# A gated recurrence with its first level ahead of the states and block copies on ScalarE, and a routing with two spreads ahead of the first pick

## The reference, cut to what matters

```python
# per head (4 heads of 128), forward and backward; f = gate, k = 1 - f
S_t = diag(f_t) S_{t-1} + k_t v_t^T          # S_0 = final state of the context
o_t = S_t^T q_t                              # o = o_forward + o_backward
out = rmsnorm(o) * silu(g)
# then: x += g1 * (concat(hyena, out) @ w_out);  h = modulate(rmsnorm(x))
aff = softmax(h @ router_w)                  # (256 tokens, 16 experts)
gates, idx = top_k(aff.T, 32)                # each expert takes its 32 tokens
y = (silu(xg @ w1) * (xg @ w3)) @ w2         # per expert, times gates, added back
```

## Time and profile before

| | us |
|---|---|
| median of three runs | 2678.49 |
| the profiled execution | 2676.36 |
| its span | 2674.3 |
| TensorE busy | 2302.1 (86%) |
| VectorE busy | 774.6 (29%) |
| ScalarE busy | 344.9 (13%) |
| mean granted TensorE clock | 0.929 |

### The profile page before, as it was taken

One profiled execution on the slowest core, in us unless ns is written; L12 is line 12 of the kernel. 1 busy time (PEld: TensorE's weight loads), 2 busy tenths in 40 slices (PEclk: granted clock), 3 DMA queues, 4 the chain that ended last, 5 costly groups with the idle time before them and its releaser, 6 DMA issues.

```text
span 2674.3 us, 34093 instructions
## 1 busy us (share of the span) xinstructions
PE 2302.1 (86%) x14956; PEld 1619.0 (61%) x14968; DVE 774.6 (29%) x1473; ACT 344.9 (13%) x618; POOL 17.5 (1%) x21
## 2 busy tenths in 40 slices
PE   7999989999999999999999999896666666666675
PEld 5888768888888789888886878652121111111221
DVE  5544534574000465511023338640000000000000
ACT  3001222002000232111002211210000000000000
POOL 1000000000000000000000000000000000000000
PEclk9999999999999999999999999988887788887778
DMA  9889235886445240044442223489999999999997
GB/s 394 343 354 379 95 142 226 354 341 256 157 141 204 90 147 20 24 169 148 136 172 78 66 77 115 189 330 428 428 427 428 426 428 427 428 427 427 426 428 338
DMA packets 70098, 709.51 MB, mean 265 GB/s; under 512 B 7776, under 2 KB 7904, under 8 KB 8672
## 3 DMA queue, kind: packets, MB, share of 16 engines
q1 hardware_dynamic: 69984, 707.79, 65.6%
HBM read 706.71 MB, written 1.05 MB: 265 GB/s over the span
## 4 chain that ended last, share of the span: by engine, by line
PE 62%; DMA 30%; DVE 7%; ACT 1%; issue 1%; SPq 0%; DVEq 0%; ACTq 0%
DMA arena<-in_experts 27%; PE ps L691 11%; PE ps L698 11%; PE ps L708 11%; PE ps L757 5%; PE ps L875 4%; PE ps L1071 4%; PE ps L1282 2%; PE ps L1314 2%; DMA ring<-in_experts 2%; PE ps L664 1%; PE ps L1069 1%; PE ps L773 1%; PE ps L1247 1%; PE ps L787 1%
## 5 line engine op out<-in xcount | busy, mean ns | idle before, releaser
L1282 PE MATMUL ps<-arena 128*32 128x512 f32 x1376 | 211.8, 748 | 147.0 <-DMA arena<-in_experts 146.5
L691 PE MATMUL ps<-hT_sq,arena 128*128 128x256 f32 x1376 | 312.1, 380 | 4.1 <-ACT hT_sq L1391 2.9
L708 PE MATMUL ps<-hid,arena 128*128 128x256 f32 x1408 | 311.1, 379 | 0.2 <-DVE hid L1796 0.2
L698 PE MATMUL ps<-hT_sq,arena 128*128 128x256 f32 x1376 | 311.0, 379 | 0.0
L708 PEld LDWEIGHTS ps<-hid,arena 128*128 128x128 f32 x1408 | 267.4, 190 | 36.9 <-issue 0.6
L691 PEld LDWEIGHTS ps<-hT_sq,arena 128*128 128x128 f32 x1376 | 260.5, 190 | 45.5 <-issue 8.5
L698 PEld LDWEIGHTS ps<-hT_sq,arena 128*128 128x128 f32 x1376 | 261.4, 190 | 35.5
L1282 PEld LDWEIGHTS ps<-arena 128*32 128x32 f32 x1376 | 42.4, 124 | 310.6 <-DMA arena<-in_experts 226.0
L1363 ACT ACTIVATE arena<-ps 128x512 f32<-128x512 f32 (+4 forms) x147 | 89.1, 615 | 946.1 <-PE ps L1293 308.5
L1796 DVE TENSOR_TENSOR hid<-sil,ps 128x256 f32<-128x256 f32 x88 | 37.0, 421 | 560.4 <-ACT sil L1415 560.2
L1757 DVE CUSTOM_DVE_ANT_0 hT_sq<-arena 128x1024 f32<-128x1024 f32 x168 | 194.5, 1221 | 0.0
(11 more groups left out here) (370 smaller groups left out, 2184.0 us busy)
## 6 DMA issues: line engine op xcount, KB each, us to landing
arena<-in_experts SPq DMA_DIRECT2D x129, 2048.0 KB, 41.1
arena<-in_ada SPq DMA_DIRECT2D x96, 1024.0 KB, 9.7
ring<-in_experts SPq DMA_DIRECT2D x42, 2048.0 KB, 40.9
ring<-in_ring_w SPq DMA_DIRECT2D x51, 1024.0 KB, 5.1
arena<-in_ffn_gate SPq DMA_DIRECT2D x44, 1024.0 KB, 6.5
arena<-in_ffn_up SPq DMA_DIRECT2D x44, 1024.0 KB, 6.2
arena<-in_ffn_down SPq DMA_DIRECT2D x44, 1024.0 KB, 4.8
hT_sq<-in_experts SPq DMA_DIRECT2D x21, 2048.0 KB, 40.4
```

The source lines that it names most:

```text
L691: last = mm(ps[:, ft, 0:T], gate3[:, kt, ft * P:(ft + 1) * P], h3[:, kt, :], start=kt == 0, stop=kt == KT - 1)
L698: last = mm(ps[:, ft, T:2 * T], up3[:, kt, ft * P:(ft + 1) * P], h3[:, kt, :], start=kt == 0, stop=kt == KT - 1)
L708: last = mm(acc(m), down3[:, ft, m * P:(m + 1) * P], hid3[:, ft, :], start=False, stop=True, skip_group_check=True)
L1282: last = mm(ps[32 * n:32 * n + 32, part, :], e_xe[:, kt, :], w[:, (kt % 2) * SLOT + n * 512:(kt % 2) * SLOT + (n + 1) * 512], start=kt == ...
```

## The change

- `hyena_back` moves ahead of the last unit of `b2_in`, on TensorE and on ScalarE.
- The first level of both directions comes first on TensorE, ahead of the context's transposes, which go to banks 0 to 3. The states are made one by one after level 0's halves. The parts beside start at level 1; `beside(12)` and `(13)` stand behind the two halves of the crossing, `(14)` and `(15)` behind the two sums of squares, where the eight filler matmuls stood.
- Level 0 doesn't scale `g_K`; `g_E` is filled and copied by halves there, behind a wait for the transposes (`hg_ctx_t`). The last level doesn't update `g_E`, which holds the product of `g_q` and `g_F` instead.
- From level 6 on (`MASKED`), ScalarE takes the scores over by block copies, two of 32 or one of 64 columns a tile, instead of VectorE's masked copy.
- The crossing's part of the output matmuls comes last within a bank. The variances of the second bank are made between the heads. Sqrt's table is loaded by a dummy before the second bank, Exp's in norm 9.
- Routing: the row copy comes ahead of the large one on ScalarE, two spreads ahead of the first pick with fillers around them, and the other 14 within expert 0.

```diff
-        x_kt = ar(B1 + 12288, 2048).rearrange("p (d t c) -> p d t c", d=2, t=TT)
-        x_v = tiles(ar(B1 + 15360, 1024), HYW)
+        x_kt = ar(B1 + 17408, 2048).rearrange("p (d t c) -> p d t c", d=2, t=TT)
+        x_v = tiles(ar(B1 + 1024, 1024), HYW)
...
+        MASKED = 6
@@ TensorE, hgrn
+                pe.wait_ge(sem("hg_gates"), 2)
+                pe.wait_ge(sem("hy_mixed"), 4)
+                for d in range(2):
+                    level(d, g_k, lambda d: g_q)
+                pe.wait_ge(sem("b2_evac"), B2_FIRST)
                 for d in range(2):
                     for tt in range(TT):
                         for h in range(HGH):
+                            last = tr(ps[:, 2 - 2 * d + tt, h * P:(h + 1) * P], x_k[:, d, h, tt * P:(tt + 1) * P], ident)
+                        last.then_inc(sem("hg_ctx_t"), 1)
...
                 for lev in range(NLEV):
                     for d in range(2):
-                        pe.wait_ge(sem("hg_taken"), 2 * lev + d + 1)
+                        if lev < MASKED:
+                            pe.wait_ge(sem("hg_taken"), 2 * lev + d + 1)
+                        else:
+                            pe.wait_ge(sem("hg_copied"), 2 * (lev - MASKED) + d + 1)
                         pe.wait_ge(sem("hg_scaled"), 2 * lev + d + 1)
-                        level(d, lambda d: g_K[:, d], lambda d: g_Q[:, d])
-                        beside(2 + 2 * lev + d)
+                        level(d, g_K if lev else g_k, lambda d: g_Q[:, d])
+                        if lev == 0:
+                            state(d)
+                        else:
+                            beside(2 * lev - 2 + d)
...
                 for b in range(2):
                     pe.wait_ge(sem("hg_os"), 2 * b + 2)
                     mm(ps[:, 4 + b, :], ones, sq[:, b * 512:(b + 1) * 512], start=True, stop=True).then_inc(sem("hg_out"), 1)
-                keep_clock(6, 8)
+                    beside(14 + b)
@@ TensorE, routing and experts
+                keep_clock(7, 2)
+                pe.wait_ge(sem("e_rows"), 3)
+                spread(range(0, 2))
+                keep_clock(7, 12)
                 pe.wait_ge(sem("e_rows"), 4)
-                spread(range(0, 8))
...
-                            spread(range(8, NE))
+                            spread(range(2, NE))
@@ ScalarE, hgrn
+                for lev in range(MASKED, NLEV + 1):
+                    hb = 1 << lev - 1
+                    for d in range(2):
+                        act.wait_ge(sem("hg_level"), 2 * lev + d + 1)
+                        for tt in range(TT):
+                            src = ps[:, 4 + 2 * d + tt, :].rearrange("p (h s) -> p h s", s=P)
+                            for lo in range(0, P, 2 * hb):
+                                early, late = (slice(lo + hb * i, lo + hb * (i + 1)) for i in ((0, 1) if d == 0 else (1, 0)))
+                                last = copy(g_A[early, d, tt, :, late], src[early, :, late])
+                        last.then_inc(sem("hg_copied"), 1)
@@ VectorE, hgrn
+                        if lev < MASKED:
+                            taken(lev, d)
+                        else:
+                            dve.wait_ge(sem("hg_level"), 2 * lev + d + 1)
+                        last = tt_(cut(g_Q[:, d], late), cut(g_q, late), cut(g_F[:, d], late), ALU.mult)
+                        if lev > 0:
+                            last = tt_(cut(g_K[:, d], early), cut(g_k[:, d], early), cut(g_E[:, d], early), ALU.mult)
+                        last.then_inc(sem("hg_scaled"), 1)
...
+                        if lev == 0:
+                            dve.wait_ge(sem("hg_ctx_t"), 4)
+                            nc.vector.memset(cut(g_E[:, d], late), 1.0)
+                            done(cp(cut(g_E[:, d], early), cut(g_F[:, d], late)))
                         dve.wait_ge(sem("hg_scaled"), 2 * lev + d + 1)
-                        done(tt_(cut(g_E[:, d], early), cut(g_E[:, d], early), edge_l, ALU.mult))
+                        if 0 < lev < NLEV:
+                            done(tt_(cut(g_E[:, d], early), cut(g_E[:, d], early), edge_l, ALU.mult))
                         done(tt_(cut(g_F[:, d], late), cut(g_F[:, d], late), edge_e, ALU.mult))
+                        if lev == NLEV:
+                            last = tt_(g_E[:, d], g_q, g_F[:, d], ALU.mult)
```

More of the change, by code:

```diff
@@ L1100, in hgrn, with level, state @@
             def hgrn():
[L1102 to L1105, removed]
+                def level(d, kk, qq):
                     for tt in range(TT):
                         for h in range(HGH):
[L1108 to L1112, removed]
+                            last = mm(ps[:, 4 + 2 * d + tt, h * P:(h + 1) * P],
+                                      kk[:, d, h, tt * P:(tt + 1) * P], qq(d)[:, h, tt * P:(tt + 1) * P],
+                                      start=True, stop=True)
+                    last.then_inc(sem("hg_level"), 1)
+                def state(d):
+                    if d == 0:
+                        pe.wait_ge(sem("hg_ctx_kt"), 4)
                     for h in range(HGH):
@@ L1117, in hgrn @@
                     last.then_inc(sem("hg_state"), 1)
[L1118 to L1120 removed]
+                pe.wait_ge(sem("hg_gates"), 2)
[4 more added lines that the diff above has]
+                for d in range(2):
                     for tt in range(TT):
                         for h in range(HGH):
[L1123 to L1131, removed]
+                            last = tr(ps[:, 2 - 2 * d + tt, h * P:(h + 1) * P], x_k[:, d, h, tt * P:(tt + 1) * P], ident)
+                        last.then_inc(sem("hg_ctx_t"), 1)
                 for lev in range(NLEV):
                     for d in range(2):
[L1135 removed]
+                        if lev < MASKED:
+                            pe.wait_ge(sem("hg_taken"), 2 * lev + d + 1)
+                        else:
+                            pe.wait_ge(sem("hg_copied"), 2 * (lev - MASKED) + d + 1)
                         pe.wait_ge(sem("hg_scaled"), 2 * lev + d + 1)
[L1137 to L1138 removed]
+                        level(d, g_K if lev else g_k, lambda d: g_Q[:, d])
[3 more added lines that the diff above has]
+                            beside(2 * lev - 2 + d)
+                pe.wait_ge(sem("hg_copied"), 2 * (NLEV - MASKED) + 1)
                 for d in range(2):
@@ L1144, in hgrn @@
                                   g_Q[:, d, h, (1 - d) * P:(2 - d) * P], start=True, stop=True)
-                last.then_inc(sem("hg_cross"), 1)
-                pe.wait_ge(sem("hg_cross_s"), 1)
-                pe.wait_ge(sem("hg_taken"), 2 * NLEV + 2)
+                    if d == 1:
+                        last.then_inc(sem("hg_cross"), 1)
+                    beside(2 * NLEV - 2 + d)
+                pe.wait_ge(sem("hg_copied"), 2 * (NLEV - MASKED) + 2)
                 pe.wait_ge(sem("hg_scaled"), 2 * NLEV + 3)
[L1149 to L1156, removed]
-                        last = mm(o[:, (1 - d) * P:(2 - d) * P], g_v[:, d, e0], g_X[:, d, h, :],
-                                  start=False, stop=d == 1, skip_group_check=True)
-                    if h % 2:
-                        last.then_inc(sem("hg_out"), 1)
@@ new lines, in hgrn @@
+                for b in range(2):
+                    for h in (2 * b, 2 * b + 1):
+                        o, e0 = half(6, h), slice(h * P, (h + 1) * P)
+                        mm(o, g_S[0][:, h, :], g_E[:, 0, h, :], start=h % 2 == 0, stop=False, skip_group_check=True)
+                        mm(o, g_S[1][:, h, :], g_E[:, 1, h, :], start=False, stop=False, skip_group_check=True)
+                        for d in range(2):
+                            for tt in range(TT):
+                                mm(o[:, tt * P:(tt + 1) * P], g_v[:, tt, e0], g_A[:, d, tt, h, :],
+                                   start=False, stop=False, skip_group_check=True)
+                    pe.wait_ge(sem("hg_cross_s"), 1)
+                    for h in (2 * b, 2 * b + 1):
+                        for d in range(2):
+                            last = mm(half(6, h)[:, (1 - d) * P:(2 - d) * P], g_v[:, d, h * P:(h + 1) * P], g_X[:, d, h, :],
+                                      start=False, stop=d == 1, skip_group_check=True)
+                    last.then_inc(sem("hg_out"), 1)
@@ L1387, in norm @@
                 root(rstd[:, :])
+                if i == 9:
+                    f(small[:, 225:226], ones[:, 0:1], ACT.Exp)
                 if shift is not None:
@@ L1581, in hgrn @@
                     f(sq3[:, 2 * b:2 * b + 2, :], g_F[:, 0, 2 * b:2 * b + 2, :], ACT.Square).then_inc(sem("hg_os"), 1)
+                    if b == 0:
+                        f(small[:, 224:225], ones[:, 0:1], ACT.Sqrt)
                 for h in range(HGH):
```

36 lines of the change are left out of this document (18 added, 18 removed).

## The result

The changed kernel takes 2656.4 us in the median of four runs (2654.79 to 2657.76), beside 2678.57 for the kernel before on the same chip. The ratio is 0.9919, 95% interval 0.9905 to 0.9933: 22.2 us or 0.8% faster, 0.9 us from the forecast.

A forecast was written before the change was run, and what follows sets the result against it. The expert load stream, started by the first weight slot's release, was taken to bound the kernel. Recurrence 17.5 plus routing 6.4 less hole 1.0 gave 22.9 us, so about 2655.5 from 2678.5; range 2648 to 2665.

The forecast's parts named there:

- this change is worth exactly what it moves the first slot's release: Expert weight stream: the span ends a fixed 918 us after load 9's wait ends at 1756.62, unless the stream tears.
- if load 9 moves by 24 and the end by less, the stream was torn: Sign of being wrong, at the expert load stream: the give-back step would then fail.
- its own bounds: Forecast's bounds on start (7.5 to 11), routing (2.4 to 7.4) and hole (0 to 3): 2649 to 2663 us.
- Recurrence: Start, levels, outputs and roots of the gated recurrence: projection starts 17.5 us earlier, at 1692.8.
- rival 3: Levels 6 and 7: ScalarE's twelve block copies are dear, above 3.1 us each making the kernel slower; chance 0.03.
- Routing: First pick and first slot: earlier row copy, fewer spreads and fillers gain 6.4 us, bounds 2.4 to 7.4.
- after the pick of expert 1 the clock was down for a while too: Routing: reason for taking 6.4 us instead of the 7.4 of full clock throughout.
- Rival 1: Routing: clock stays at 1.2 GHz through the pick, only 2.4 of 6.4 us arrives, 2659.5; chance 0.14.
- What is given back: Expert 0: six more spreads and ranks (9.0 us) delay load 17, leaving a 1.0 us hole in the stream.
- 1.0 + p: Hole ahead of load 17 with the whole landing lead; p is the extra time from a slower TensorE clock.
- its wait grows from 3.08 to about 11: Expert 0: TensorE's wait for the gated product, in us, behind six more ranks on VectorE.
- Rival 2: Behind expert 0's wait TensorE restarts at half clock: hole 6 to 11 us, time 2660.5 to 2665.5; chance 0.14.

The follow-up runs named there:

- x11: Changed kernel with the context's transposes and states ahead of the first level, as before the change; 2665.14 us, ratio 0.9949.
- x6: Changed kernel with VectorE's masked copy at all levels, none of ScalarE's block copies; 2658.99 us, ratio 0.9926.
- x10: Kernel before with 23 filler matmuls in TensorE's two waits ahead of the recurrence's output matmuls; 2676.02 us, ratio 0.9995.
- x2: Kernel before with the routing part of the change alone; 2674.52 us, ratio 0.9988.
- x7: Changed kernel with expert 0's gated product ahead of the last four ranks on VectorE; 2652.05 us, ratio 0.9909.
- x3: Changed kernel with six spreads in place of the twelve routing fillers, leaving eight for expert 0; 2658.67 us, ratio 0.9925.
- x5: Changed kernel without its fourteen filler matmuls in the routing; 2661.59 us, ratio 0.9935.
- x12: The changed kernel measured once more, unaltered; 2656.63 us, ratio 0.9921.
- x4: Changed kernel with the fourteen spreads behind the second half of expert 0's matmuls instead of between the halves; 2662.74 us, ratio 0.9943.
- x8: Changed kernel with 24 filler matmuls between the last expert's four last slots; 2655.16 us, ratio 0.9914.
- x9: Changed kernel with both the edits of x7 and x8; 2652.97 us, ratio 0.9910.

## Why the prediction was right

**The bound held up to the last landing.** In all fourteen profiles load 191 lands 905.3 us behind load 9, plus the lag's excess over 39.2 where there is one, within 0.2 us. The end comes 12.3 to 15.6 behind that. So "this change is worth exactly what it moves the first slot's release", less the hole, is shown for the last landing; behind it up to 3.3 us depend on the clock.

**The signs that it named came.** The first level's mask starts 10.4 us earlier with respect to the gates' end (2.5 instead of 12.8 behind it), there are 20 masked copies instead of 28, and the outputs start without idle time at clock 1.00. One sign of being wrong came too: "if load 9 moves by 24 and the end by less, the stream was torn". It was torn, by 1.53, for which the sum had 1.0. The range is wider at its lower end than its own bounds give: the best of each, 22.9 + 1.6 + 1.0 + 1.0 = 26.5, lead to 2652, not 2649. The measured time lies within either.

**Recurrence, 17.5 forecast, 17.38 measured.** Level 1 at 1624.44 for 1624.1, outputs at 1678.96 for 1678.8, release of loads 2 to 5 at 1687.96 for 1687.7, projection at 1692.94 for 1692.8. The fill and copy of E took 0.85, for 0.9 taken. The block copies were 0.27 to 0.33 for 0.3, and rival 3 falls: it needed 3.1 each. x11 shows the order at the start as a cause (5.7), x6 the block copies (3.2), x10 the clock in the outputs (2.6). These make 11.5; that the other 5.9 come from the parts beside, the fill of E and the table load moved off the path is argued from the timelines, and no run undoes one of them alone.

**Routing, 6.4 forecast, 7.42 measured** (24.80 less 17.38). This term was too small by 1.0: the discount "after the pick of expert 1 the clock was down for a while too" was not due, and the bound for 2.4 GHz throughout, 7.4, is what came. Yet the discount was no mere caution: x2, x7 and x11, with the same fillers, lost 1.6 to 3.0 between load 8 and load 9. That the changed kernel lost none of it is in part luck. Rival 1 did not happen in the changed kernel; x3 and x5 show that it would have, without the fillers (load 9 at 1737.58 and 1737.29), 5.8 and 5.5 late, where its two bounds are 5.0 apart. x5 was 5.2 slower than the changed kernel; x3 only 2.3, since its profile has neither the hole nor the slow last slot (1.5 and 1.6 us).

**What is given back, 1.0 forecast, 1.53 measured.** The step's rule, 1.0 + p, holds: TensorE had 11.37 of work between the wait and load 17 instead of 10.94, so p = 0.4. The six ranks cost 8.9 (the restart came 29.41 behind load 9, before 20.50) for 9.0. One number within it was wrong: "its wait grows from 3.08 to about 11" measured 7.75. Its own terms give 9.3 (3.08 and 9.0, less 2.8 for the spreads). The other 1.5 is that the spreads ran at half clock from 1741 on (28 instructions in 8.17, where 16 took 3.71 before), so that part 1 ended later and more of the ranks lay under TensorE's own work. The sum is the same, since VectorE's end decides.

Rival 2 falls, for another reason than the prediction's. It argued that before, "after 3.08 us of waiting the whole 10.94 still passed near full speed". It didn't. The group behind the gated product starts at half clock in both kernels, and at full clock only in x7, behind a wait of 0.91. Before, a window behind the restart of the earlier trace rows and the end of the slow part:

```profile
1778.00:1779.00 1.00, 1.00 (x5) 0.86 (x5) 0.00 (x0) 0.60 (x1) 0.00 (x0) 0.50 1.08 459
```

```profile
1780.52 2.05 PE L1257 MATMUL ps<-con,vec 128*128 128x128 f32 x16
```

The changed kernel, and x7:

```profile
1762.00:1763.00 1.00, 1.00 (x6) 0.76 (x5) 0.00 (x0) 0.60 (x1) 0.00 (x0) 0.50 1.08 459
```

```profile
1765.06 2.05 PE L1271 MATMUL ps<-con,vec 128*128 128x128 f32 x16
```

```profile
1755.10 0.63 PE L1307 MATMUL ps<-con,arena 128*128 128x128 f32 x4 [0.91 <-DVE arena L2295]
1755.65 1.58 PE L1271 MATMUL ps<-con,coef 128*64 128x128 f32 x16
1757.16 2.05 PE L1271 MATMUL ps<-con,vec 128*128 128x128 f32 x16
```

From the restart to the row at L1257 or L1271 with `vec` are 3.40 us before, 3.83 in the changed kernel and 2.06 in x7. So a restart at half clock costs 1.8, and 1.3 of that was already in the 10.94; only the difference is p. That p came near nothing was right, but the row given for it was misread. By the rule in the Trainium skill's "TensorE: Matmul & The Clock Gate" ("HAM oscillation — how this bites in real kernels") the group starts cold after a wait. The trace agrees that it does, in both kernels; the "at least a few microseconds" that the prediction drew from it did not come.

**Not foreseen: 1.57 at the end.** The last slots' matmuls swing between 1.92 and 2.9 to 3.6, mostly from one slot to the next, in both kernels. Before, load 191's fell on a full one, after on a half one. Nothing in the sum stood for it. It offset the 1.0 that was too little in the routing: 17.38 + 7.42 - 1.53 - 1.57 = 21.7, for 22.9. The forecast of the time is thus partly right by two errors of 1.0 and 1.57, which cancel but for 0.5; the hole's 0.5 and 0.1 in the recurrence are the rest. This is the account of one execution of each kernel, and both lie under their medians, by 2.2 and 1.6; the medians give 22.2. x12 shows 14.0 behind the landing again; how often the kernel before ends in 12.4 is not known.

**Open.** What makes the same fillers hold the clock in one kernel (changed, x4, x6, x8, x9, x12: load 9 within 11.2 to 11.4 of load 8) and not in another (x2 14.2, x11 13.3, x7 12.8) was not tried. In x2 it fell within the pick, in x7 and x11 about its end, so that their first slots began at 0.50. x7 gives TensorE the same instructions as the changed kernel up to there, and its pick began at 1724.49, x4's at 1724.51, and x4 kept the clock. So neither the program nor the time of the start explains it there.

## What to carry to other kernels

Where a kernel ends in a stream of loads that never pauses, find the one release that starts it and measure a change by that instant alone. Then ask how much later the next release in the ring may come before the queue runs dry, and push deferred work into that slack and no further: here six more ranks (8.9) and a slightly slower restart (0.4) put 9.3 us into a slack of 7.8, and putting the gated product ahead of the last four ranks closed the hole of 1.5. What comes behind the last landing has to be looked at by itself. Where a short chain of thin matmuls lies on the path, the wait ahead of it is better filled with full-size matmuls than with thin ones, even useful ones; look at the granted clock afterwards, since in three of the nine profiles with these fillers it fell all the same.

## What the runs showed of the hardware

- TensorE's clock fell to half while TensorE was busy throughout, with matmuls on weights of 16 partitions (x3: 5.00 of 5.00 busy, granted 0.50), and stayed at full with 128-partition bf16 fillers in the same place, in six of the nine profiles that have them.
- A restart at half clock (granted 0.50) cost about the same behind waits of 3.08, 7.75 and 15.96 us: 10.94, 11.37 and 11.26 us from the restart to load 17 (before, changed, x4). Its first 20 matmul instructions took 3.40, 3.83 and 3.72 us, and 2.06 at full clock behind a wait of 0.91 (x7). The shorter pick ran wholly at half clock, 7.01 for 3.73, in x5 behind a wait of 3.02.
- The queue of 2 MB loads has a sharp edge. With eight asked for ahead of it (loads 9 to 16), a ninth asked for 34.2 us behind the first or sooner costs nothing, and at 40.7 to 47.5 us the lag beyond 39.2 is lost one for one.
- ScalarE copies 128 elements on 32 partitions out of a bank in 0.27 and 256 on 64 in 0.33; 256 on all partitions took 0.33 too.
